# One-core hybrid decoder block: the time side of the chunked recurrence on partition halves, crossing products on all four 64x64 quadrants

## The reference

```
def step(state, inp):                      # per head, per token; state is 64 x 64
    r_t, w_t, k_t, v_t, kk_t, a_t = inp
    sa = einsum('bhvk,bhk->bhv', state, -kk_t)
    state = state * w_t + sa (x) (kk_t * a_t) + v_t (x) k_t
    y_t = einsum('bhvk,bhk->bhv', state, r_t)
```

## Time and profile before

| | us |
|---|---|
| median of 3 runs | 2943.32 (2942.22 to 2951.57) |
| the profiled execution | 2941.55, span 2939.7, mean granted clock 0.97 |
| PE busy | 2859.6 (97%) |
| DVE busy | 1246.1 (42%) |
| ACT busy | 862.2 (29%) |
| POOL busy | 194.0 (7%) |
| recurrence | from 833.4 to 1072.9 in the span |

### The profile page before, as it was taken

One profiled execution on the slowest core, in us unless ns is written; L12 is line 12 of the kernel. 1 busy time (PEld: TensorE's weight loads), 2 busy tenths in 40 slices (PEclk: granted clock), 3 DMA queues, 4 the chain that ended last, 5 costly groups with the idle time before them and its releaser, 6 DMA issues.

```text
span 2939.7 us, 47500 instructions
## 1 busy us (share of the span) xinstructions
PE 2859.6 (97%) x18428; PEld 2310.2 (79%) x18428; DVE 1246.1 (42%) x1713; ACT 862.2 (29%) x1250; POOL 194.0 (7%) x224
## 2 busy tenths in 40 slices
PE   6999999999889999999999999999999999999997
PEld 4867777777579975888888888888888888888886
DVE  5354445554555543334332334223432234333544
ACT  4334343434322222332221222212221122233333
POOL 3000000000022311110000000000000000011110
PEclk7999999999889987999999999999999999999998
DMA  5443444344331122333333333333333333333333
GB/s 176 134 122 122 150 144 138 106 136 129 104 119 42 55 74 65 98 95 93 100 93 100 93 100 93 100 93 100 93 100 93 100 93 100 93 100 105 95 96 89
DMA packets 505237, 303.45 MB, mean 103 GB/s; under 512 B 23325, under 2 KB 483765, under 8 KB 504125
## 3 DMA queue, kind: packets, MB, share of 16 engines
q1 hardware_dynamic: 481021, 270.02, 31.6%
q10 hardware_dynamic: 18976, 14.71, 1.6%
q0 software_dynamic: 5152, 17.40, 1.5%
HBM read 265.79 MB, written 36.31 MB: 103 GB/s over the span
## 4 chain that ended last, share of the span: by engine, by line
issue 59%; PE 33%; POOL 4%; DVE 2%; DMA 1%; ACT 1%; SPq 0%; POOLq 0%; DVEq 0%; ACTq 0%
PE acc L525 6%; PE acc L527 6%; PE acc L526 6%; PE bank L665 4%; POOL sumsq L1526 2%; PE bank L599 1%; PE bank L586 1%; POOL nm L1557 1%; PE acc L665 1%; PE bank L615 1%; PE bank L625 1%; PE bank L592 1%; PE bank L673 1%; PE bank L674 1%; PE bank L783 0%
## 5 line engine op out<-in xcount | busy, mean ns | idle before, releaser
L1143 DVE TENSOR_TENSOR w_lo<-w_raw,w_hi 128x1024 fp32r<-128x1024 f32 (+1 forms) x422 | 515.7, 1222 | 1312.9 <-ACT w_hi L850 1311.7
L525 PE MATMUL acc<-a_hi,w_hi 128*128 128x512 f32 x2080 | 826.3, 397 | 5.2 <-DVE a_lo L1410 5.0
L850 ACT ACTIVATE w_hi<-w_raw 128x1024 fp32r<-128x1024 f32 x420 | 445.2, 1060 | 1302.7 <-PE acc L527 1283.1
L526 PE MATMUL acc<-a_lo,w_hi 128*128 128x512 f32 x2080 | 816.5, 393 | 0.0
L527 PE MATMUL acc<-a_hi,w_lo 128*128 128x512 f32 x2080 | 816.5, 393 | 0.0
L525 PE MATMUL acc<-b_hi,w_hi 128*128 128x512 f32 x1280 | 498.5, 389 | 0.0
L526 PE MATMUL acc<-b_lo,w_hi 128*128 128x512 f32 x1280 | 498.0, 389 | 0.0
L527 PE MATMUL acc<-b_hi,w_lo 128*128 128x512 f32 x1280 | 498.0, 389 | 0.0
L525 PEld LDWEIGHTS acc<-a_hi,w_hi 128*128 128x128 f32 x2080 | 394.7, 190 | 100.4 <-issue 12.9
L527 PEld LDWEIGHTS acc<-a_hi,w_lo 128*128 128x128 f32 x2080 | 394.4, 190 | 83.2
L526 PEld LDWEIGHTS acc<-a_lo,w_hi 128*128 128x128 f32 x2080 | 394.9, 190 | 82.6 <-issue 1.9
(11 more groups left out here) (272 smaller groups left out, 2245.2 us busy)
## 6 DMA issues: line engine op xcount, KB each, us to landing
w_raw<-in_w_ff SPq DMA_DIRECT2D x256, 512.0 KB, 3.9
w_raw<-in_w_in SPq DMA_DIRECT2D x100, 512.0 KB, 3.6
w_raw<-in_w_out SPq DMA_DIRECT2D x32, 512.0 KB, 3.8
w_raw<-in_w_ple_gate SPq DMA_DIRECT2D x32, 512.0 KB, 3.8
z_d<-ev POOLq DMA_DIRECT2D x50, 256.0 KB, 3.2
ab_d<-ab ACTq DMA_DIRECT2D x8, 1024.0 KB, 4.7
x<-ab_d SPq DMA_DIRECT2D x8, 1024.0 KB, 4.8
xin<-in_x SPq DMA_DIRECT2D x16, 256.0 KB, 2.7
```

Source lines behind the costliest of these rows:

```text
L525: mm(dst, wh, hi[:, kt, :], start=kt == 0, stop=False)
L526: mm(dst, wh, lo[:, kt, :], start=False, stop=False)
L850: A(w_hi[:, s, :, :], w_raw[:, s, :, :], ACT.Copy).then_inc(sg("w_hi_ready"), 1)
L1143: V.tensor_tensor(w_lo[:, s, :, 0:width], w_raw[:, s, :, 0:width], w_hi[:, s, :, 0:width].bitcast(F32), ALU.subtract).then_inc(sg("w_split ...
```

## The change

Time-side tiles get another layout: their partition half is no longer the head within the pair, but half of the pairs' list. A time tile holds head m of group `tp` such that the products that go from features to times (`to_time`) and back (`to_features`) take, for each j, all four combinations of feature half and time half, that is all four 64x64 quadrants; each combination of a source half goes to its own PSUM bank. Products of times with times (`within`) stay on two opposite quadrants, as the state's part of y does. The state and ec are indexed by `feature(n)` and strided slices accordingly.

The transposes of v, b and k are 128-wide (`turn`), four transposes each into a whole bank, the third inside level 2; ScalarE copies them out, 128x512 at a time, with the columns permuted. The transposed first factor isn't a transpose any more: the product of x4's kinds 0 and 2 is formed the other way round (`n_turned`) and masked with a new constant (C_LVT), to which ones are added.

In a level VectorE adds ones to pt as it leaves PSUM (q = pt + 1), and TensorE multiplies q instead of pt; its results are then the new xs and xt, so ScalarE copies them out (four copies a level) and VectorE adds nothing. r is split: the v term (r2) is multiplied in level 2 and copied by ScalarE in level 3, the state term (r1) is multiplied in level 4, and VectorE adds them there. The state's part of y goes to a bank of its own; VectorE copies it to y_all and adds the other part, which ScalarE's copy did before. Both masks of a kind wait for one count over both groups. The feature store writes ab_d with kind outside pair, in pieces of 64 floats instead of 256.

```
+    c[:, C_LVT:C_LVT + C] = (j[:, None] == t[None, :] + 1) & (j[:, None] % 2 == 1)
...
-    ab_d = dram("ab_d", (NC, P, NPAIR, 4, C))
+    ab_d = dram("ab_d", (P, NC, 4, NPAIR, C))
...
+    gram, wide, side_by, whole = bank[0:2], bank[2:4], acc, bank[4:6]
+    heads = (slice(0, HD), slice(HD, P))
...
+            def within(g, dst, lhs, rhs):
+                for j in range(H):
+                    for tp in heads:
+                        last = mm(low(dst)[tp, j, :], lhs(tp, g * H + j), rhs(tp, g * H + j), start=True, stop=True)
                 return last
+            def to_time(dst, lhs, rhs, n=C):
+                for j in range(H):
+                    for q, tp in enumerate(heads):
+                        for g, ph in enumerate(heads):
+                            last = mm(dst[g][tp, j * n:(j + 1) * n], lhs(ph, 2 * j + q), rhs(ph, 2 * j + q), start=True, stop=True)
+                return last
+            def to_features(dst, lhs, rhs, start=True):
+                for j in range(H):
+                    for q, tp in enumerate(heads):
+                        for g, ph in enumerate(heads):
+                            last = mm(low(dst[q])[ph, j, :], lhs(tp, g * H + j), rhs(tp, g * H + j), start=start and j == 0, stop=not start and j == H - 1)
+                return last
+            def turn(dst, src):
+                for j in range(H):
+                    last = nc.tensor.transpose(dst[:, j * P:(j + 1) * P], src[:, 2 * j:2 * j + 2, :].rearrange("p n t -> p (n t)"), ident)
+                last.then_inc(sg("turned"), 1)
...
+                to_time(gram, lambda ph, n: x[ph, 2, n, :], lambda ph, n: x[ph, 0:2, n, :], P).then_inc(sg("products_done"), 1)
+                pe.wait_ge(sg("y_taken"), 2 * c + 2)
+                to_time(side_by, lambda ph, n: x[ph, 0, n, :], lambda ph, n: x[ph, 2, n, :]).then_inc(sg("n_turned"), 1)
+                pe.wait_ge(sg("state_ready"), 2 * c + 2)
+                to_time(wide, lambda ph, n: x[ph, 3, n, :], lambda ph, n: x[ph, 0:2, n, :], P).then_inc(sg("products_done"), 1)
+                turn(whole[0], v[:, :, :])
+                turn(whole[1], x[:, 2, :, :])
...
+                        wait("n_ready", 5, lv, g)
+                        if lv == 1:
+                            wait("xt0_ready", 1, 1, g)
+                        else:
+                            wait("xt_ready", 4, lv - 1, g)
+                        within(g, gram[g], lambda tp, m: nm[tp, lv - 1, m, :], lambda tp, m: xt[tp, m, :]).then_inc(sg("pt_done"), 1)
+                    if lv == 2:
+                        pe.wait_ge(sg("turns_taken"), 3 * c + 1)
+                        turn(whole[0], x[:, 3, :, :])
+                        pe.wait_ge(sg("turns_taken"), 3 * c + 2)
+                        for m in range(NPAIR):
+                            for tp in heads:
+                                last = mm(m3(whole[1])[tp, m, :], gk[tp, m, 0, :], vt[tp, m, :], start=True, stop=True)
+                        last.then_inc(sg("r2_done"), 1)
+                    if lv == 4:
+                        pe.wait_ge(sg("turns_taken"), 3 * c + 3)
+                        pe.wait_ge(sg("r2_taken"), c + 1)
+                        to_time(whole, lambda ph, n: x[ph, 0, n, :], lambda ph, n: state[ph, feature(n), :]).then_inc(sg("r1_done"), 1)
                     for g in range(2):
-                        wait("pt_ready", g, 5, lv)
-                        wait("x_ready", g, 6, lv)
+                        wait("q_ready", 5, lv, g)
+                        if lv == 1:
+                            wait("x0_ready", 1, 1, g)
+                            wait("products_ready", 2, 2, g)
+                        else:
+                            wait("x_ready", 5, lv - 1, g)
                         if lv < 5:
-                            if lv == 1:
-                                wait("transposes_taken", g, 3, 2)
-                            each(g, gbank[g][3][:, 0:H * C], lambda ph, n: xs[ph, old, n, :], lambda ph, n: pt[ph, n, :], "dxt_done")
-                        if lv == 1:
-                            wait("transposes_taken", g, 3, 1)
-                        each(g, gbank[g][2][:, 0:H * C], lambda ph, n: pt[ph, n, :], lambda ph, n: xs[ph, old, n, :], "dx_done")
+                            within(g, side_by[g], lambda tp, m: xs[tp, old, m, :], lambda tp, m: qt[tp, m, :]).then_inc(sg("xt_done"), 1)
+                        within(g, wide[g], lambda tp, m: qt[tp, m, :], lambda tp, m: xs[tp, old, m, :]).then_inc(sg("x_done"), 1)
...
+                wait("r_ready", 1, 1)
+                for n in range(NPAIR):
+                    for ph in heads:
+                        mm(m3(whole[0])[ph, feature(n), :], state[ph, feature(n), :], x[ph, 1, n, :], start=True, stop=True)
...
+                wait("xt_ready", 4, 4)
+                to_features(side_by, lambda tp, m: vt[tp, m, :], lambda tp, m: gk[tp, m, 1, :])
+                if c < NC - 1:
+                    to_features(wide, lambda tp, m: ktm[tp, m, :], lambda tp, m: vt[tp, m, :])
+                    wait("sa_ready", 1, 1)
+                    to_features(wide, lambda tp, m: bt[tp, m, :], lambda tp, m: sa[tp, m, :], start=False).then_inc(sg("s_done"), 1)
+                wait("sa_ready", 1, 1)
+                to_features(side_by, lambda tp, m: sa[tp, m, :], lambda tp, m: gb[tp, m, 1, :], start=False).then_inc(sg("y_multiplied"), 1)
...
-                    act.dma_start(ab_d[:, :, bass.ds(i, 1), :, :].rearrange("c p a k t -> p c (a k t)"), ab[:, :, :, :].rearrange("p c k t -> p c (k t)")).then_inc(sg("features_stored"), 16)
+                    act.dma_start(ab_d[:, :, :, bass.ds(i, 1), :].rearrange("p c k a t -> p (c k) (a t)"), ab[:, :, :, :].rearrange("p c k t -> p (c k) t")).then_inc(sg("features_stored"), 16)
...
+                turned(0)
+                turned(1)
+                for lv in range(1, 6):
+                    if lv == 3:
+                        turned(2)
+                        act.wait_ge(sg("r2_done"), c + 1)
+                        A(r2[:, :, :], m3(whole[1][:, :]), ACT.Copy).then_inc(sg("r2_taken"), 1)
                     for g in range(2):
-                        wait("transposes_done", g, 3, k + 1)
-                        A(dst[:, pairs[g], :], half(g, (2, 3, 0)[k]), ACT.Copy).then_inc(sg("transposes_taken"), 1)
-                transposed(0)
-                transposed(1)
-                for lv in range(1, 6):
-                    for g in range(2):
-                        wait("pt_done", g, 5, lv)
-                        A(pt[:, pairs[g], :], half(g, 1), ACT.Copy).then_inc(sg("pt_ready"), 1)
-                    if lv == 1:
-                        transposed(2)
+                        if lv < 5:
+                            wait("xt_done", 4, lv, g)
+                            A(xt[:, pairs[g], :], low(side_by[g]), ACT.Copy).then_inc(sg("xt_ready"), 1)
+                        wait("x_done", 5, lv, g)
+                        A(xs[:, lv % 2, pairs[g], :], low(wide[g]), ACT.Copy).then_inc(sg("x_ready"), 1)
...
+                masked(gb, gram, 0)
+                dve.wait_ge(sg("n_turned"), c + 1)
                 for g in range(2):
+                    level0(g, xt[:, pairs[g], :], low(side_by[g]), C_LVT, "xt0")
+                for g in range(2):
+                    wait("xt0_masked", g, 1, 1)
+                    ones(g, xt[:, pairs[g], :], xt[:, pairs[g], :]).then_inc(sg("xt0_ready"), 1)
+                masked(gk, wide, 1)
                 for g in range(2):
                     wait("products_ready", g, 2, 1)
+                    level0(g, xs[:, 0, pairs[g], :], gb[:, pairs[g], 0, :], C_LVL, "x0")
                 for g in range(2):
+                    wait("x0_masked", g, 1, 1)
+                    ones(g, xs[:, 0, pairs[g], :], xs[:, 0, pairs[g], :]).then_inc(sg("x0_ready"), 1)
                 for lv in range(1, 6):
                     for g in range(2):
+                        wait("pt_done", g, 5, lv)
+                        ones(g, qt[:, pairs[g], :], low(gram[g])).then_inc(sg("q_ready"), 1)
+                    if lv == 4:
+                        dve.wait_ge(sg("r1_done"), c + 1)
+                        dve.wait_ge(sg("r2_taken"), c + 1)
+                        for g in range(2):
+                            V.tensor_tensor(rr[:, pairs[g], :], low(whole[g]), r2[:, pairs[g], :], ALU.add).then_inc(sg("r_ready"), 1)
                 if c < NC - 1:
+                    dve.wait_ge(sg("s_done"), c + 1)
+                    for q in range(2):
+                        V.tensor_tensor(sn[:, pairs[q], :], st[:, c % 2, pairs[q], :], low(wide[q]), ALU.add).then_inc(sg("state_summed"), 1)
+                    for q in range(2):
+                        wait("state_summed", q, 1, 1)
+                        V.tensor_tensor(st[:, (c + 1) % 2, pairs[q], :], sn[:, pairs[q], :], ec[:, q::2, c:c + 1].broadcast_to([P, H, C]),
                                         ALU.mult).then_inc(sg("state_ready"), 1)
```

(27 more changed lines are left out.)

109 lines of the change are left out of this document (30 added, 79 removed).

## The result

The changed kernel takes 2952.1 us (median of 20 runs) against 2942.4 for the kernel before (20 runs, same chip): a ratio of 1.0029, 95% interval 1.002 to 1.0037, +8.5 us by the ratio. It is slower, by a little less than forecast. The profiled execution took 2953.4 us where that of before took 2941.55.

A forecast was written before the change was run, and what follows sets the result against it. TensorE bound the kernel before; afterwards VectorE's chain would bound each chunk's start, TensorE the rest. Chunks +0.6, switches +2.4 and clock +8.8 make +11.8 on 2941.55, 2953.4; the median, 1.8 higher, 2955, range 2938 to 2970.

The forecast's parts named there:

- gb to TensorE's return: Chunk start, from VectorE's first gb mask until q of level 1 lets TensorE go on at 11.35 us.
- TensorE's return to sn: Rest of the chunk, levels 1 to 5 and end groups, bound by TensorE: 18.58 us before switches and clock.
- VectorE's chain as the bound: Chunk start: VectorE's in-order operations up to q of level 1 take about 11 us, leaving TensorE idle some 4.6.
- The exclusive port: Rule weighed for VectorE beside GpSimd: the blocked operation takes 1.15 us, 10 us more in all; measured 0.945 was used.
- The eight operations ahead of gb: Chunk start on VectorE: two each of sn, st, y copies and y sums, 8 x 0.35 = 2.80 us.
- The crossing pace: Products between features and times on four quadrants: 17 ns a 64-column record, between 14.6 and 29.1.
- The rival in which four quadrants give nothing: Crossing products stay at 29.1 ns for 64 columns; 31.47 us a chunk, 2967 in all; chance 0.24.
- Switches: TensorE changing between 64x64 tiles and whole-array transposes, two a chunk on the path: 0.15 us each, +2.4 in all.
- The clock: TensorE's granted clock falls to 0.50 after each chunk's idle piece: 1.1 us a chunk, +8.8 in all.
- Store: Feature store in four times as many, shorter pieces: hidden by the loops, taken as 0, once 0 to +5 us.
- the signs named ahead: Trace features that would show the forecast right, such as VectorE's chain of about 11 us and TensorE's idle gap.
- The rival "faster": Chunk start: VectorE's six SBUF operations do not meet GpSimd, chain 3.1 us shorter, clock holds; -22, 2921; chance 0.09.

The follow-up runs named there:

- nm-late run: Changed kernel, but GpSimd makes the nm products of levels 2 to 5 only after the second x0_ready; ratio 0.9946 to the kernel before.

## Why the prediction was right

The profiled executions differ by 11.8 us (2953.38 less 2941.55), the sum of the forecast to the tenth. That is luck in part: the terms were off on both sides. For a chunk the forecast was 29.93 + 0.30 + 1.1 = 31.33, the trace has 31.46. Means of the seven chunks by stretch, in us:

| stretch | forecast | measured |
|---|---|---|
| gb to TensorE's return | 11.35 - 2.52 = 8.83 | 7.87 |
| TensorE's return to sn | 18.58 - 0.28 + 0.30 + 1.1 = 19.70 | 20.82 |
| sn to gb | 2.80 | 2.78 |

- **VectorE's chain as the bound:** right. It runs without a pause, TensorE waits for it, and shortening it or its company shortens the chunk. Its size was off: -0.96. The mis-sized term is 0.87 an operation beside GpSimd: the three pairs took 1.40, 1.22 and 1.72 us from start to next start, where 1.74 each was forecast. Four of the six operations took 0.94 us, the first xt0 plus ones 0.60 and the first x0 mask 0.43, although GpSimd was at work beside them too. That GpSimd is the cause, the nm-late run showed. The exclusive port of the Trainium skill ("SBUF — State Buffer", section "SBUF: two separate sides"), weighed as 1.15 us an operation, was not seen here either: none of the six took over 0.95.
- **The eight operations ahead of gb:** 2.66 where nothing waits, I took 2.80: -0.14.
- **The crossing pace:** 14.6 ns, I took 17. 128 records between the return and sn: -0.3. The rival in which four quadrants give nothing fell with the first rows; so did the rule of the Trainium skill ("TensorE: Matmul & The Clock Gate", section "Wait — 56ns, not 53.3ns?") of some 25 ns from start to start, if it is meant for records on different quadrants: 13.6 and 14.6 were measured.
- **Missing:** the stalls, +0.4 a chunk on the path. The forecast gave the crossing its burst pace without asking what supplies the instructions. They ate all that the fast pace gained on 17 ns.
- **Switches:** 0.17 each by the rows (964.44, 965.46), I took 0.15.
- **The clock:** its fall was forecast, its price was too small: 1.9 a chunk and not 1.1, +0.8. The forecast took two stretches of 3.3 us with 2.0 of them in idle time, and then half of that. A stretch of 3.4 us lies wholly behind the return in four of the seven chunks, and a stretch of 6.8 reaches 4.6 to 6.1 us past it in the other three.
- **Store:** 0, confirmed alone.

These make 31.33 - 0.96 - 0.14 - 0.3 + 0.4 + 0.04 + 0.8 = 31.17; 0.3 us a chunk stay unassigned. So the mechanism was right, and the agreement to the tenth comes from a chain that was sized too long against a clock that was sized too cheap and a stall that was not foreseen. Of the signs named ahead, the chain of about 11 us was 10.2 (sn to q), the gap of 4 to 5 was 3.84, crossing groups of 0.5 to 0.6 were 0.47, and levels near 3.0 were right (level 3 took 3.08, 978.54 to 981.62).

The rival "faster" needed more than four of the six operations clear of GpSimd. They were not; in the nm-late run all six were short, 0.41 to 0.61 us, and the kernel became faster indeed, as its condition said. Why the first gb falls anywhere between 831.9 and 841.3 in the profiles here, though the code ahead of it is the same in all but two, stays open; no run was made for it.

## What to carry to other kernels

A change that frees the bounding engine is worth what the next chain leaves of it, so write that chain out operation by operation, with who works beside it: here one wait on GpSimd turned +9 us into -16, and work off the chain counts only behind the point where the chain is bound anew. A gap in TensorE's work costs its own length and then the clock: here 3.84 us idle cost 1.9 us more behind the gap. A kernel can be faster with useless products in it, though these need instructions too. Where several small matmuls run side by side, count instructions too, not only columns.

## What the hardware showed that was not expected

- Instruction supply: 128 records (256 instructions with their weight loads) come with each packet of 16384 bytes; in a long run on four quadrants that work at 14.6 ns, 128 records of 64 columns took 3.46 us, 27 ns a record. All 93 stalls above 0.5 us in the traces end 1.2 to 1.6 us behind the end of a packet.
- Beside GpSimd four of VectorE's six operations with both operands in SBUF took 0.94 us and two 0.43 and 0.60, though GpSimd never paused; alone they take 0.41. GpSimd's own went from 0.73 to 0.90.
- Records of one pair of quadrants start while those of the other, issued before, still run: 16 and 16 in 0.59 us, where one pair after the other would take 0.93.
- Stores in 256-byte pieces landed in 6.9 instead of 4.7 us, and the one queued behind in 9.9 instead of 5.4.
